# The way from the first norm to the experts: the shared block's passes between the transposes, the residual copies one per expert, the shared product behind the choice of experts, the gate slots one block later

## What is computed

```python
def _swiglu(x, wg, wu, wd):
    return (jax.nn.silu(x @ wg) * (x @ wu)) @ wd

def _moe(x, router_w, router_b, wg, wu, wd, sg, su, sd):
    xf = x.reshape(B * T, D)
    s = jax.nn.sigmoid((xf @ router_w).astype(jnp.float32))
    sb = s + router_b.astype(jnp.float32)
    gscore = jnp.sum(lax.top_k(sb.reshape(-1, N_GROUPS, EXPERTS_PER_GROUP), TOP_K)[0], axis=-1)
    gsel = jnp.argmax(gscore, axis=-1)
    ...
    wsel = wsel / jnp.sum(wsel, axis=-1, keepdims=True)
    gate = jnp.sum(jax.nn.one_hot(idx, N_EXPERTS, dtype=jnp.float32) * wsel[..., None], axis=1)
    out = _swiglu(xf, sg, su, sd).astype(jnp.float32)
    for e in range(N_EXPERTS):
        out = out + gate[:, e:e + 1] * _swiglu(xf, wg[e], wu[e], wd[e]).astype(jnp.float32)
    return out.astype(x.dtype).reshape(B, T, D)
```

## Time and profile before

| | us |
|---|---|
| median of 3 runs | 1082.61 |
| lowest and highest | 1082.49, 1086.24 |
| the profiled execution, its own time | 1087.75 |
| its span, first to last instruction | 1086.0 |
| busy in it: PE (matmul), DVE, ACT | 1023.6, 827.3, 660.3 |

### The profile page before, as it was taken

The page is one execution under the profiler, slowest core; times in us unless marked ns, Lnnn a source line. Parts: engine busy times, 40 slices in busy tenths (PEclk is TensorE's granted clock), DMA queues, the critical chain, the costliest instruction groups (busy, mean ns, idle before and its releaser), DMA issues. The chain is left out here.

```text
span 1086.0 us, 24604 instructions
## 1 busy us (share of the span) xinstructions
PE 1023.6 (94%) x10126; PEld 786.3 (72%) x10126; DVE 827.3 (76%) x1484; ACT 660.3 (61%) x1059; POOL 0.7 (0%) x10
## 2 busy tenths in 40 slices
PE   6999999999998799999999999999999978999995
PEld 4877777777776699965567777777777658999443
DVE  4786677654898699989887766676559877999886
ACT  5565455754365777767767445556534676777764
POOL 0000000000000000000000000000000000000000
PEclk9999999999999899999999999999999998999998
DMA  9754444323462389988735534443244415999861
GB/s 348 268 167 143 140 142 129 108 98 116 156 235 78 114 299 327 333 281 312 280 118 192 165 122 137 141 139 98 98 136 156 155 45 187 332 324 328 294 260 51
DMA packets 59653, 205.06 MB, mean 189 GB/s; under 512 B 7088, under 2 KB 10348, under 8 KB 59020
## 3 DMA queue, kind: packets, MB, share of 16 engines
q1 hardware_dynamic: 55980, 195.96, 53.2%
q10 hardware_dynamic: 3552, 7.42, 1.9%
HBM read 198.77 MB, written 3.40 MB: 186 GB/s over the span
## 5 line engine op out<-in xcount | busy, mean ns | idle before, releaser
L1042 DVE SCALAR_TENSOR_TENSOR wlo<-w,whi 128x1024 f16<-128x1024 f32 x358 | 429.7, 1220 | 76.9 <-ACT whi L549 75.3
L549 ACT ACTIVATE whi<-w 128x1024 f16<-128x1024 f32 x358 | 370.6, 1049 | 93.6 <-PE bank L1732 52.2
L1732 PE MATMUL bank<-xhi,whi 128*128 128x320 f16 x704 | 211.0, 300 | 0.0
L1732 PE MATMUL bank<-xhi,wlo 128*128 128x320 f16 x704 | 210.5, 299 | 0.0
L1732 PE MATMUL bank<-xlo,whi 128*128 128x320 f16 x704 | 210.5, 299 | 0.0
L1732 PE MATMUL bank<-arena_b,whi 128*128 128x128 f16 x2048 | 183.4, 222 | 0.0
L1732 PE MATMUL bank<-arena_b,wlo 128*128 128x128 f16 x1024 | 179.2, 222 | 0.0
L1732 PEld LDWEIGHTS bank<-arena_b,whi 128*128 128x128 f16 x2048 | 160.0, 99 | 0.0
L1732 PEld LDWEIGHTS bank<-arena_b,wlo 128*128 128x128 f16 x1024 | 101.6, 99 | 0.0
L1732 PEld LDWEIGHTS bank<-xhi,whi 128*128 128x128 f16 x704 | 68.8, 98 | 30.3 <-issue 2.5
L1732 PEld LDWEIGHTS bank<-xhi,wlo 128*128 128x128 f16 x704 | 68.9, 98 | 26.8
(11 more groups left out here) (357 smaller groups left out, 1751.6 us busy)
## 6 DMA issues: line engine op xcount, KB each, us to landing
w<-in_w SPq DMA_DIRECT2D x358, 512.0 KB, 4.7
arena_b<-head_rows ACTq DMA_DIRECT2D x2, 1920.0 KB, 7.2
xT<-in_x SPq DMA_DIRECT2D x2, 640.0 KB, 4.9
out_y<-xT SPq DMA_DIRECT2D x4, 320.0 KB
rows<-in_rows ACTq DMA_DIRECT2D x1, 1024.0 KB, 11.3
rows<-in_rows SPq DMA_DIRECT2D x1, 1024.0 KB, 5.8
out_ckv<-arena_a SPq DMA_DIRECT2D x2, 320.0 KB
acc<-kr SPq DMA_DIRECT2D x2, 288.0 KB
```

Source lines behind the costliest of these rows:

```text
L549: A(whi[:, n % SLOTS, :], w32[:, n % RAW, :], ACT.Copy, scale=WS).then_inc(hi_done.sem, 1)
L1042: V.scalar_tensor_tensor(wlo[:, n % SLOTS, :], w32[:, n % RAW, :], WS, whi[:, n % SLOTS, :], ALU.mult, ALU.subtract).then_inc(lo_done.sem, 1)
L1732: ins = M(out, w[:, s, sub * P:(sub + 1) * P], rhs(part, k), start=(n == 0), stop=(n == 3 * len(subs) - 1))
```

## The change

The work is the same; it stands in another order.

- PE: the 24 passes of block U0+3 are cut into eight lots of three, one behind each transposed bank n = 3 to 10. The choice counts (L2151) stand behind n = 4 with its lot. The wait for `most_set` moves behind the last transpose. The first gather waits for eleven banks to be out and the second for twelve, instead of both for twelve. The gate slots (`gate_slots`) move from before the first expert to behind its first block, and the first expert's gate rows from behind j = 0 to behind j = 2.
- ACT: the first shared Tanh stands ahead of the split of U0+4, the splits of U0+5 and U0+6 behind all transposed banks. The eight residual copies leave this place: one stands in each of the first eight experts (`acc_start(e)`). After the branch come the four gather evictions with the gates' high half between them, then `gate_hi`, the split of U0+7, and only then the two shared halves.
- DVE: the low half of U0+4 stands ahead of the wait for the counts instead of behind the one-hot matrix. The first shared product (`hidden_product`, the first part of `hidden`) stands right behind the gates. `gate_lo` and the low half of U0+7 come before the rest of the shared expert.

```diff
@@ ACT
                 a.then_inc(r_e.sem, 1)
-                hi_lead(U0 + 1)
-                x_tokens(0)
...
                 shared_tanh(0)
-                for j in range(1, 4):
+                hi_lead(U0 + 1)
+                for j in range(4):
                     x_tokens(j)
-                    if j < 3:
-                        hi_lead(U0 + 1 + j)
-                for c in range(KD):
+                hi_lead(U0 + 2)
+                hi_lead(U0 + 3)
+
+                def acc_start(c):
                     a = A(acc[:, c * T:(c + 1) * T], xT[:, c * T:(c + 1) * T], ACT.Identity,
                           scale=ALPHA / XS, bias=par_a[:, C_L1B + c:C_L1B + c + 1])
-                a.then_inc(acc_pre.sem, 1)
+                    if c == KD - 1:
+                        a.then_inc(acc_pre.sem, 1)
...
                     for q in range(4):
                         if q == 2:
                             gates_hi()
-                            shared_hi(0)
...
+                    act.wait_ge(g_tr.sem, g_tr.value(l, 1))
+                    A(gate_hi[0:EXPERTS, :], bank[4][0:EXPERTS, :], ACT.Copy).then_inc(g_hi.sem, 1)
+                    hi_lead(U0 + 4)
+                    shared_hi(0)
                     act.wait_ge(u_free.sem, u_free.value(l, 1))
                     shared_tanh(1)
-                    act.wait_ge(g_tr.sem, g_tr.value(l, 1))
-                    A(gate_hi[0:EXPERTS, :], bank[4][0:EXPERTS, :], ACT.Copy).then_inc(g_hi.sem, 1)
                     shared_hi(1)
-                    hi_lead(U0 + 4)
...
                                     hi_e(4)
+                                    if e < KD:
+                                        acc_start(e)
@@ DVE
+                lo_lead(U0 + 1)
 
                 dve.wait_ge(pos_ps.sem, pos_ps.value(l, 1))
...
-                lo_lead(U0 + 1)
...
+                hidden_product(0, U0 + 2, 0, T, None)
                 dve.wait_ge(most_set.sem, most_set.value(l, 1))
-                lo_lead(U0 + 2)
                 dve.wait_ge(gt_h.sem, gt_h.value(l, 1))
...
+                lo_lead(U0 + 2)
                 lo_lead(U0 + 3)
 
                 def shared_lo():
-                    for f in range(2):
-                        hidden(f, U0 + (2 * f + 2), f, T, f * T, None)
+                    hidden_lo(0, T, 0, None)
+                    hidden_product(1, U0 + 4, 1, T, None)
+                    hidden_lo(1, T, T, None)
...
-                    shared_lo()
-
                     dve.wait_ge(g_hi.sem, g_hi.value(l, 1))
                     V.tensor_tensor(gate_lo[0:EXPERTS, :], bank[4][0:EXPERTS, :], gate_hi[0:EXPERTS, :],
                                     ALU.subtract).then_inc(g_lo.sem, 1)
                     lo_lead(U0 + 4)
+                    shared_lo()
@@ PE
+                    if 2 < n < 11:
+                        k = n - 3
+                        for w, xp in ((whi, 0), (whi, 1), (wlo, 0)):
+                            a = M(bank[UPB[3]][:, 0:T], w[:, slot(l, U0 + 3), k * P:(k + 1) * P], x_rhs(xp, k),
+                                  start=(k == 0 and w is whi and xp == 0), stop=(k == KD - 1 and w is wlo))
+                        if k == KD - 1:
+                            a.then_inc(blk_done.sem, 1)
+                    if n == 4:
...
                     for q in range(4):
-                        if q >= 2:
+                        if q < 2:
+                            pe.wait_ge(xt_ev.sem, xt_ev.value(l, 11 + q))
+                        else:
                             pe.wait_ge(xg_ev.sem, xg_ev.value(l, q - 1))
                         gather(5 + q % 2, 0, q)
...
+                                        if e == 0 and j == 0:
+                                            gate_slots()
+                                        if j == (0 if e else 2):
```

More of the change, by code:

```diff
@@ L1000, in _ @@
                         act.sem_inc(s_.sem, n)
+                    for c in range(KD):
+                        acc_start(c)
                     gates_hi()
@@ L1576, in _, with hidden_product @@
                                 ALU.mult).then_inc(g_sel.sem, 1)
-                def hidden(n, ready1, f, W, c0, gate):
+                def hidden_product(n, ready1, f, W, gate):
                     dve.wait_ge(u_tanh.sem, u_tanh.value(l, n + 1))
@@ L2127, in _ @@
                     lo_passes(b, s)
[L2128 to L2145 removed]
+                ready(l, U0 + 3)
+                for n in range(12):
+                    part, half, t0 = n // 6, n // 3 % 2, min(n % 3 * P, T - P)
+                    if n == 0:
+                        pe.wait_ge(r_e.sem, r_e.value(l, 1))
+                    if n >= 3:
+                        pe.wait_ge(xt_ev.sem, xt_ev.value(l, n - 2))
+                    for c in range(4):
+                        a = M(bank[4 + n % 3][:, c * P:(c + 1) * P],
+                              (xlo if part else xhi)[:, 4 * half + c, t0:t0 + P], EYE, start=True,
+                              stop=True)
+                    a.then_inc(xt_ps.sem, 1)
+                    if 2 < n < 11:
[6 more added lines that the diff above has]
+                    if n == 4:
                         pe.wait_ge(gm_set.sem, gm_set.value(l, 1))
@@ L2184, in gather, with gate_slots @@
                     a.then_inc(xg_ps.sem, 1)
-                fits = pe.value_load(most_i[0:1, 0:1]) < CAP + 1
-                with pe.If(fits):
-                    pe.wait_ge(xt_ev.sem, xt_ev.value(l, 12))
-                    pe.wait_ge(oh_set.sem, oh_set.value(l, 1))
-                    for q in range(4):
-                        if q >= 2:
-                            pe.wait_ge(xg_ev.sem, xg_ev.value(l, q - 1))
-                        gather(5 + q % 2, 0, q)
+                def gate_slots():
                     pe.wait_ge(gt_l.sem, gt_l.value(l, 1))
@@ L2201, in _ @@
                     a.then_inc(g_tr.sem, 1)
+                pe.wait_ge(most_set.sem, most_set.value(l, 1))
+                fits = pe.value_load(most_i[0:1, 0:1]) < CAP + 1
+                with pe.If(fits):
+                    pe.wait_ge(oh_set.sem, oh_set.value(l, 1))
+                    for q in range(4):
+                        if q < 2:
+                            pe.wait_ge(xt_ev.sem, xt_ev.value(l, 11 + q))
+                        else:
+                            pe.wait_ge(xg_ev.sem, xg_ev.value(l, q - 1))
+                        gather(5 + q % 2, 0, q)
                     for gg in range(0, GROUPS // 2):
```

22 lines of the change are left out of this document (3 added, 19 removed).

## The result

| us | before | after |
|---|---|---|
| median of 8 runs each, on one chip | 1084.45 | 1077.51 |
| lowest and highest | 1079.08, 1087.5 | 1072.87, 1079.81 |
| the profiled execution's span | 1086.0 | 1077.8 |

The ratio is 0.994, with a 95% interval of 0.9916 to 0.9964: faster by 6.9 us where 7.2 was predicted. The median of 1077.5 itself lies 2.1 us above the forecast of 1075.4, since that started from 1082.61, the median of three runs of before, and eight runs have 1084.45; it is just inside the forecast's own range (to 1077.8). All of layer 0's stage lies 1.83 us earlier in this trace than in that of before (first transpose at 348.38 instead of 350.21), so I compare times counted from each layer's first transpose.

A forecast was written before the change was run, and what follows sets the result against it. DVE paces the dense experts, so time won before its first expert product should reach the end: 4.8 - 1.2 (clock) = 3.6 us per layer, twice 7.2; 1082.6 - 7.2 = 1075.4 us. Own range 1073.0 to 1077.8; 8 in 10: 1071.5 to 1081.5.

The forecast's parts named there:

- Passes between transposes: PE's transposes with three passes behind each bank: PE no longer waits and ends at 357.0 instead of 358.4.
- The split of U0+4 in DVE's gap: DVE's 1.22 us split fills its 1.26 us wait for L2151, so the gates end at 360.1 instead of 361.3.
- The first gather eviction: On ACT, with the residual copies gone: starts at 359.5, 3.5 us earlier than 363.04; last eviction ends at 362.4.
- rival 3: PE's clock falls from the first gathers on, delaying the gate slots: 1.9 us lost per layer, 1086.4 us; chance 0.10.
- What is late next: After the gathers: slots done at 365.4, ACT waits 3.0 us, first expert product at 375.2 instead of 380.00.
- The walk: Timing of PE, ACT and DVE from the router to the first expert product, which comes 4.8 us earlier per layer.
- PE's new wait: Ahead of expert 1, PE waits 2.8 us for block U0+8, until 373.0.
- The clock: PE restarts at expert 1 after its new wait, partly at 1.2 GHz: 1.2 us lost per layer, between 0 and 2.4.
- The signs: Profile checks, including first product at 375.2, then period 6.27 us; wrong if DVE's period grows in experts 0 to 7.
- Copies: One 0.46 us residual copy per expert before ACT's 1.31 us wait costs nothing; that wait falls to 0.85 us.
- rival 2: Residual copies in the first eight experts are not hidden: 7.4 us come back, 1082.8 us; chance 0.10.
- Rival 1: Transfers bound the experts, so only the weight stream's earlier restart counts: 1.3 us per layer, 1080.0 us; chance 0.12.

The follow-up runs named there:

- e3_passes_whole: Changed kernel with block U0+3's 24 passes in one piece again, behind the ninth transposed bank; median 1080.35 us, ratio 0.9973 to the kernel before.
- e4_copies_back: Changed kernel with the eight residual copies back on ACT ahead of the branch; median 1088.94 us, ratio 1.0055 to the kernel before.
- e9_before_fill: Kernel before with 12 unread products added in PE's 2.0 us wait before the first expert; median 1081.35 us, ratio 0.9986 to the kernel before.
- e1_fill: Changed kernel with 18 unread products added in PE's new wait before expert 1; median 1074.45 us, ratio 0.9922 to the kernel before.
- e13_four_copies: e12_late_slots with the residual copies four each in the first two experts, not one in each of eight; median 1070.26 us, ratio 0.9868 to before.
- e6_shared_ahead: Changed kernel with gate slots first and U0+7's split and shared-expert work ahead of the wait for them; median 1069.16 us, ratio 0.9868 to before.
- e8: Kernel before with only the residual copies moved, one into each of the first eight experts; median 1076.49 us, ratio 0.9943 to the kernel before.
- e2: Changed kernel with only the gate slots moved back ahead of the first expert's first block; median 1071.23 us, ratio 0.9885 to the kernel before.
- e12_late_slots: e6_shared_ahead's order but with the gate slots one block later, as in the change; median 1067.16 us, ratio 0.9864 to the kernel before.
- e10_copies_back_fill: e4_copies_back with 34 unread products added in PE's 5.0 us wait ahead of the third gather; median 1085.18 us, ratio 1.0009 to the kernel before.

## Why the prediction held, point by point

Its times are those of the old trace; 1.83 us are taken off to compare.

- **Passes between transposes**: PE's last bank at 355.2 by the working, 355.1 measured; one PE wait of 0.24 us in the transposes instead of none. Worth 1.6 us per layer by itself (e3_passes_whole).
- **The split of U0+4 in DVE's gap**: gates done at 358.27, measured 358.33.
- **The first gather eviction**: 357.67 against 357.55, the last one's end 360.57 against 360.34. The new small waits of 1.5 and 0.9 us were 1.42 and 0.78, and the clock stayed at 1.00 through them, so rival 3 did not occur here. Its mechanism did in e4_copies_back, around the wait of 5.03 us.
- **What is late next**: slots done 363.57, ACT's gate copy at 363.56 after a wait of 3.22 (3.0); the second shared half at 366.66 (366.8); first expert product 373.37 against 373.34. The walk's 4.8 us were 4.83 and 4.92. What it did not see is that in these traces 1.9 of them were the clock's: it put full-clock durations for expert 0's blocks where before had run them at the lower level, and never named this as a gain. It also said that nothing in the stretch depends on the profiled execution being 5.1 us above the median; e9_before_fill, whose stage won 3.8 us and whose median 1.6, speaks against that. Against e9_before_fill's 27.94 the order alone is worth 3.0 us.
- **PE's new wait**: 2.8 predicted, 2.88 measured.
- **The clock**: 1.2 us per layer between ends 0 and 2.4; measured 2.01 and 0.45, 2.46 together against 2.4. The mechanism was right (e1_fill): the 3.1 us of delay at the full low level and the 0.7 us of slack behind it measure 3.0 and 0.9 (last section). But how long the level stayed low was not predicted, and the sum is right as the mean of two unequal cases, which rests on chance as much as on the choice. The rule quoted from the Trainium skill, TensorE: Matmul & The Clock Gate (A second HAM failure mode: psum-queue depth-cycling), gave 2.4 in each layer: nearly so in layer 0, not in layer 1.
- **The signs**: the list asked for a period of 6.27 us behind the first product and called the prediction wrong if a period grew in experts 0 to 7. Expert 0's did, to 8.28 and 6.72. This is the clock's term of the prediction's own sum, which the list forgot; in experts 1 to 7 no period grew.
- **Copies**: hidden, with the 0.85 us that was forecast; rival 2 fell. Their limit was shown by e13_four_copies.
- **Rival 1, the transfers**: fell. In e6_shared_ahead the first product comes 8 us earlier than before in each layer, and the periods of the experts are still 6.26 to 6.27 (every fourth 6.99): the stream of weights did not hold them up.
- **What the prediction left out** is a price for the late slots as such. It walked through the wait for them as given and did not ask what the kernel would do without it. By the runs, the 4.83 us of layer 0 are: copies 3.9 (e8), passes 1.6 (e3), slots minus 2.2 (e2), and a remainder of 1.5; in layer 1 4.2, 1.6, minus 2.4 and 1.5. The remainder would be the first shared product behind the choice and DVE's order; I did not isolate it. The parts were undone from different ends, and the copies' figure holds the clock's 1.9 us too, so the remainder is a difference, not a measurement.

## What to carry to other kernels

When a product comes late, don't price its delay by itself: list what stands behind its waiter on that engine and doesn't need it, and move that ahead; here 2.2 to 2.4 us per layer became nothing (e12_late_slots). Small work that is needed much later costs nothing in front of a wait that recurs, up to about the length of that wait (one copy of 0.45 us under 1.31 was free, four made the next instruction 0.39 us late and the period grew by 0.38). A walk from durations must say at which clock each was taken: in these traces 1.9 us of a 4.8 us gain were TensorE's return to 2.4 GHz, and filling a wait with products that nobody reads shows this part within one run. A stage's time from one profiled execution holds that execution's clock: compare it with the medians before you call it the kernel's.

## What the hardware did that I had not expected

The price of one and the same wait of TensorE varies. In four kernels PE waits 2.9 us ahead of expert 1, and the first period grows by anything from 0 to 2.01 us. The granted clock in the 6 us from PE's restart explains it. The rows of both layers after, of layer 0 in e10_copies_back_fill, and of layer 0 in e4_copies_back (columns as in the earlier trace rows):

```profile
371.30:377.30 6.00, 6.00 (x58) 6.00 (x58) 5.83 (x8) 4.42 (x7) 0.00 (x0) 0.50 0.80 264
903.63:909.63 6.00, 6.00 (x85) 6.00 (x86) 5.83 (x8) 4.95 (x7) 0.00 (x0) 0.78 0.79 246
```

```profile
375.26:381.26 6.00, 6.00 (x79) 6.00 (x80) 5.83 (x8) 4.50 (x6) 0.00 (x0) 0.72 0.78 255
```

```profile
378.87:384.87 6.00, 6.00 (x108) 6.00 (x109) 5.83 (x8) 4.69 (x8) 0.00 (x0) 1.00 0.76 259
```

| run, layer | granted clock | 6 x (1 - clock), us | growth of the period, us |
|---|---|---|---|
| after, 0 | 0.50 | 3.0 | 2.01 |
| after, 1 | 0.78 | 1.3 | 0.45 |
| e3_passes_whole, 0 | 0.76 | 1.4 | 0.56 |
| e3_passes_whole, 1 | 0.72 | 1.7 | 0.81 |
| e10_copies_back_fill, 0 and 1 | 0.72, 0.72 | 1.7, 1.7 | 0.82, 0.79 |
| e4_copies_back, 0 and 1 | 1.00, 1.00 | 0, 0 | 0, 0.01 |

The third column is the time that PE loses. Where the clock fell, the period grows by about 0.9 us less: that is the slack before ACT's Tanh waits for PE (an estimate from these rows). So the price behind the restart is regular, and what varies between executions and layers is how much of the stretch is run at 1.2 GHz, and whether any is.

A wait of 2.56 us ahead of the second gathers was followed by slots at 1.2 GHz in layer 0 of e9_before_fill and not in layer 1; one of 2.56 us, ahead of the scatter matrix, was followed by full clock in layer 0 of e8_copies_alone, and one of 2.22 us at the same place in layer 1 by the lower level. In the runs read here, no fall of the clock in this stage came with waits of 1.4 us or less alone. The Trainium skill, TensorE: Matmul & The Clock Gate (What's actually happening), says that the point at which the clock changes is not tied to the kernel's own start and that the count of slow products differs between runs of one kernel. The spread measured here agrees with it.
